# Stick-breaking scores from copies on both row halves, and the conv's last 24 products added by accumulating transfers

## Chip, core and metric

One core of one Trainium2 chip runs the whole program in one launch. The metric is the device time in microseconds (us) of that launch; lower is better. TensorE (PE, with its weight loads PEld), VectorE (DVE), ScalarE (ACT), GpSimd (POOL) and the transfer queue of SyncE (SP) run beside each other and meet only at semaphores.

## What is computed

Two transformer blocks of width 1024 on 512 tokens. The change lies in the mixer of the first block:

```python
# conv branch: 512 channels, 31 taps, causal, depthwise
u = u_val * sigmoid(u_gate)
u = silu(layernorm(causal_depthwise_conv(u, conv_w, conv_b)))
# attention branch, 8 heads of 64
z = (q / 8) @ k.T                       # causal, blocks of 128 queries
log_keep  = where(causal, log_sigmoid(-z), 0)
log_after = cumsum(log_keep, reverse) - log_keep
a = where(causal, exp(log_sigmoid(z) + log_after), 0)
o = a @ v
merged = sigmoid(g_conv) * (u @ w_conv_out) + sigmoid(g_att) * (o @ w_att_out)
```

## The kernel before

All tiles hold features or keys on the 128 partitions and the 512 tokens along the free axis. Nearly every product is made of three matmuls, since each float32 operand is held as a rounded high half and a low rest (`_hi`, `_lo`): high by high, high by low, low by high (`mul`, L1758 to L1761). The engines' orders are written out by hand.

**Weights.** SP issues one 512 KB panel after another in the order of `ITEMS` into three buffers (`raw`, L446). A panel's issue waits until the panel three places before it has been used up. ACT copies a panel to `w_hi` (`prepare`, L584), DVE subtracts to get `w_lo` (`feed`, L1073), and this subtraction frees the buffer. Among the panels from gates 8 on, every gates panel is followed by one panel of `ada`, which DVE multiplies in place (L1067).

**Scores.** `scores(n)` on PE writes the scores of head n for four key blocks: against 512, 384, 256 and 128 queries. First come four small bf16 matmuls that lay down the mask (L1908), then 12 matmuls with 64 partitions of contraction, rows 0 to 63 of the array for an even head and 64 to 127 for an odd one. Head n's queries and keys stand in those partitions of `qk_hi` and `qk_lo`.

**The order in the heads.** PE, in step n: `suffix_sums(n)` (L1928), `stick_out(n-1)` (the product with V), one gates tile, `scores(n+2)`. The last two steps have no scores, and `stick_out(7)` stands at the end, before gates 9 to 15. ACT, in step h: exponential and high half of the weights of head h (`weight`, L701, L705), high half of the output of head h-1 (L630), one `w_hi`, the gates tile out of PSUM (L710), three conv products (L672), then `soft(h+2)` (L690 to L693), which waits for `z_done`. DVE, in step h: `softplus(h+1)` (L1267 to L1273), `feed` of one gates panel (and, late in the heads, an `ada` panel ahead of it), low half of the weights of head h (L1296), low half of the output of head h-1 (`head_lo`, L1278), then conv taps (L1183).

**The conv.** Two of its four channel tiles are made by DVE, one fused multiply-add for each tap (`taps`): 16 beside the q and k projection, 7 beside V, 4 in each head, and the last 7 after the heads, in the step of gates 9. The other two tiles are made by ACT, which writes one product into one of three `tap_buf` (`products`), and POOL, which adds it to `conv` (L494): 33 products before the first head's step, 21 in the heads, 4 after them, 2 at gates 9. After gates 11 PE takes the mean of all four tiles (L1982), and the layer norm follows from there.

Block 2 has the layout that the change brings to block 1 already in its last six score maps (`softmax_scores`, from n = 10): copies of q and k in the other 64 partitions (`q_twin2`, `k_twin2`), brought by POOL's queue, and matmuls on both row halves issued in turn (L2162).

Of the kernel before, what the change touches and what calls it, by code (L numbers as in the profile page):

```python
# [5 lines left out]
P = 128  # L6
D = 1024
SEQ = 512
# [18 lines left out]
WIDE = P * NB * (NB + 1) // 2  # L27
FIRST_ADA = 16
X_ACT = 5
TWIN_FROM = HEADS + 2  # L30
# [72 lines left out]
def build(nc, t):  # L103
# [4 lines left out]
    with ctx:  # L108
# [68 lines left out]
        x_sq = [place(f"x_sq{k}", [P, SEQ], f32, at=A0 + 75 * K + 2 * K * k) for k in range(KT)]  # L177
        qk_hi = place("qk_hi", [P, 8, SEQ], f32r, at=A0)
        qk_lo = place("qk_lo", [P, 8, SEQ], f32r, at=A0 + 16 * K)
        v_hi = place("v_hi", [P, NB, SEQ], f32r, at=A0 + 32 * K)  # L180
# [56 lines left out]
        def sem(name):  # L237
# [19 lines left out]
        glu_done, glu_sig, u_ready = sem("glu_done"), sem("glu_sig"), sem("u_ready")  # L257
        mod_one, mod_ready, pool_tap = sem("mod_one"), sem("mod_ready"), sem("pool_tap")
        tap_prod = sem("tap_prod")
        hi_of = {n: sem(f"hi_of_{n}") for n in ("qk1", "v1", "qk2", "v2", "v3", "qk3")}  # L260
# [6 lines left out]
        out_done_of = {n: sem(f"out_done_{n}") for n in ("ffn_out1", "ffn_out2", "wout_a", "wout_b")}  # L267
        silu_of, prod_of, act_hi_of, act_lo_of = (
            {n: sem(f"{what}_{n}") for n in ("ffn_in1", "ffn_in2")} for what in ("silu", "prod", "act_hi", "act_lo"))
        quad_in = [sem(f"quad_in{i}") for i in range(2)]  # L270
# [21 lines left out]
        lam_dot, lam_exp = sem("lam_dot"), sem("lam_exp")  # L292
        both_in, row_in = sem("both_in"), sem("row_in")
        twin2_in = [sem(f"twin2_in{i}") for i in range(2)]
        s_last = sem("s_last")
# [89 lines left out]
        def _(sp):  # L385
# [25 lines left out]
            def both_halves(n):  # L411
# [10 lines left out]
                for to, src, tile in ((k_both[upper, :], m_hi, k_tile), (k_both[lower, :], m_lo, k_tile),  # L422
                                      (q_both[upper, :], m_hi, q_tile), (q_both[lower, :], m_hi, q_tile)):
                    sp.dma_start(to.bitcast(f32), src[rows, tile, :].bitcast(f32)).then_inc(both_in, 16)

            for q, (name, i) in enumerate(ITEMS):
                if (name, i) in BOTH_AT:
                    both_halves(BOTH_AT[name, i])
                if (name, i) == ("wo", 5):
                    pair_in(0, 0)  # L430
                if (name, i) == ("ffn_in1", 1):
                    sp.wait_ge(mg_c, KT)
                    sp.dma_start(x[:], t["x"]).then_inc(x_again, 16)
# [21 lines left out]
        def _(pool):  # L455
# [34 lines left out]
            for n, (c, j) in enumerate(SUM_ORDER):  # L490
                pool.wait_ge(tap_prod, n + 3)
                if n >= 2:
                    pool.wait_ge(pool_tap, n - 1)
                nc.gpsimd.tensor_tensor(conv[:, c, :], conv[:, c, :], tap_buf[n % 3][:], ALU.add).then_inc(pool_tap, 1)  # L494

# [5 lines left out]

            pool.wait_ge(act_lo_of["ffn_in1"], FT)
            nc.gpsimd.memset(sel_f[:], 0.0).then_inc(consts2, 1)
# [57 lines left out]
        def _(act):  # L561
# [105 lines left out]
            def products(n):  # L667

                for c, j in SUM_ORDER[tapped[0]:tapped[0] + n]:
                    if tapped[0] >= 3:  # L670
                        act.wait_ge(pool_tap, tapped[0] - 2)
                    nc.scalar.activation(tap_buf[tapped[0] % 3][:], u_pad[:, c, j:j + SEQ], ACT.Copy,  # L672
                                         scale=col("conv_w", c * TAPS + j)).then_inc(tap_prod, 1)
                    tapped[0] += 1
# [9 lines left out]
            def soft(h):  # L684
                zb = 3 * (h % 2)
                act.wait_ge(z_done, h + 1)
                if h:
                    act.wait_ge(sp_ready, h)
                for c, lo, up in BY_KEY:
                    nc.scalar.activation(sb_e[:, lo:up], ps[:, zb + c, 0:up - lo], ACT.Abs).then_inc(z_abs, 1)  # L690
                act.wait_ge(z_abs, 3 * (h + 1))
                link(nc.scalar.activation(sb_e[:], sb_e[:], ACT.Exp, scale=-1.0))
                nc.scalar.activation(sb_e[:], sb_e[:], ACT.Ln, bias=1.0).then_inc(z_exp, 1)  # L693
# [95 lines left out]
            def ffn_in(s):  # L789
# [3 lines left out]
                def split(i):  # L793
                    act.wait_ge(prod_of[name], i + 1)
                    nc.scalar.activation(act_hi[:, i, :], act_f[:, i, :], ACT.Copy).then_inc(act_hi_of[name], 1)

# [4 lines left out]
                for i in range(PLAIN):  # L801
# [3 lines left out]
                    used(name, 2 * i)  # L805
                    nc.scalar.activation(t_buf[i % 2][:], ps[:, 2 * i, :], ACT.Silu).then_inc(silu_of[name], 1)
                    prepare(name, 2 * i + 1)
# [237 lines left out]
        def _(dve):  # L1045
# [243 lines left out]
            for h in range(HEADS):  # L1289
# [7 lines left out]
                if h:  # L1297
                    head_lo(h - 1, qk_hi, qk_lo, o_hi, o_ready)
                taps(4)
            head_lo(HEADS - 1, qk_hi, qk_lo, o_hi, o_ready)  # L1300
# [63 lines left out]
            def ffn_in(s):  # L1364
# [4 lines left out]
                def split_lo(i):  # L1369
                    dve.wait_ge(act_hi_of[name], i + 1)  # L1370
                    nc.vector.tensor_tensor(act_lo[:, i, :], act_f[:, i, :], act_hi[:, i, :].bitcast(f32),
                                            ALU.subtract).then_inc(act_lo_of[name], 1)

# [23 lines left out]
                for i in range(PLAIN):  # L1397
# [9 lines left out]
                    dve.wait_ge(silu_of[name], i + 1)  # L1407
                    nc.vector.tensor_tensor(act_f[:, i, :], ps[:, 2 * i + 1, :], t_buf[i % 2][:], ALU.mult)\
                        .then_inc(prod_of[name], 1)
                    if i < 2:  # L1410
# [10 lines left out]
                def product(j):  # L1421
                    dve.wait_ge(part_silu, 2 * (pairs0 + j) + SILU_C21)
                    dve.wait_ge(part_sum, 3 * (pairs0 + j) + C22)
                    nc.vector.tensor_tensor(act_f[:, PLAIN + j, :], up[:], t_buf[j % 2][:], ALU.mult)\
                        .then_inc(prod_of[name], 1)

# [3 lines left out]
                for j in range(BY_SEVEN):  # L1430
# [19 lines left out]
                    dve.wait_ge(part_out, 4 * n + P1_OUT)  # L1450
                    dve.wait_ge(prod_of[name], PLAIN + max(j - 1, 0))
                    nc.vector.tensor_tensor(t_buf[j % 2][:, 0:TOK], ps[:, bank_c, 0:TOK], sq[0][:, 0:TOK], ALU.add)\
# [3 lines left out]
                    dve.wait_ge(part_out, 4 * n + U2_OUT)  # L1456
                    dve.wait_ge(prod_of[name], PLAIN + j)
                    nc.vector.tensor_tensor(up[:, 0:TOK], ps[:, bank_b, 0:TOK], sq[0][:, TOK:SEQ], ALU.add)\
# [9 lines left out]
                product(BY_SEVEN - 1)  # L1468
                dve.wait_ge(prod_of[name], FT)
                link(nc.vector.memset(acc[:], 0.0))  # L1470
# [286 lines left out]
        def _(pe):  # L1757
# [144 lines left out]
            def scores(n):  # L1902
# [15 lines left out]

# [105 lines left out]
            def ffn_in(s, n):  # L2024
# [40 lines left out]

                pe.wait_ge(prod_of[name], 2)
                for j in range(BY_SEVEN):
# [30 lines left out]
            def ffn_out(name, ins_name):  # L2098
                for m in range(KT):
                    for k in range(FT):  # L2100
# [3 lines left out]
                        if m == 0:  # L2104
                            pe.wait_ge(act_lo_of[ins_name], k + 1)
                        if k == 0:
                            pe.wait_ge(prod_of[ins_name], PLAIN if m < 2 else FT)
                        ins = mul(ps[:, OUT_BANK[m], :], panel(name, i, P * part),
# [305 lines left out]
```

## Time and profile before

| | us |
|---|---|
| Median of 3 runs | 1373.14 |
| Lowest, highest of them | 1372.88, 1377.71 |
| The profiled execution | 1373.36 |
| Its span, as the trace has it | 1371.6 |

```profile
PE 1345.3 (98%) x7758; PEld 1168.3 (85%) x7758; DVE 990.5 (72%) x1389; ACT 712.9 (52%) x1167; POOL 176.4 (13%) x165
PE   9999999999999999999999999999999999999997
DVE  6899899678587887878425775667797788776322
POOL 2479333200010000004000011121000000000000
```

The first line gives each engine's busy time, its share of the span and its instructions. The others cut the span into 40 slices of 34 us; a digit is the busy share in tenths, 9 for 90% and more. A matmul's end is modelled in the trace, so the starts of two neighbours say more than their lengths. The chain that ended last is for 82% on PE and for 12% on DVE.

### The profile page before, as it was taken

How to read it: one execution, taken by the hardware profiler on the slowest of the kernel's cores; microseconds unless marked ns; L12 is line 12 of the kernel's file. 1: busy time of each engine (PE TensorE's matmuls, PEld its weight loads, DVE VectorE, ACT ScalarE, POOL GpSimd, SP SyncE). 2: the span in 40 equal slices, each digit the busy share in tenths (PEclk: the TensorE clock that was granted, in tenths of full speed). 3: DMA queues.
4: the chain of work that ended last, by engine and by line, in shares of the span. 5: the costliest groups of instructions: out<-in, count | busy, mean ns of one | idle time of the engine just before them, and what ended most of it. 6: DMA issues, size and time to landing. Idle time of an engine off the chain costs nothing.

```text
span 1371.6 us, 19741 instructions
## 1 busy us (share of the span) xinstructions
PE 1345.3 (98%) x7758; PEld 1168.3 (85%) x7758; DVE 990.5 (72%) x1389; ACT 712.9 (52%) x1167; POOL 176.4 (13%) x165
## 2 busy tenths in 40 slices
PE   9999999999999999999999999999999999999997
PEld 6888887788769999998887778888778999998885
DVE  6899899678587887878425775667797788776322
ACT  3466786563465555564224443557565555564221
POOL 2479333200010000004000011121000000000000
PEclk9999999999999999999999999999999999999998
DMA  9423112456801232224522144543221323223221
GB/s 348 166 81 104 47 47 73 129 185 197 306 16 62 93 116 100 96 105 151 186 94 92 62 138 116 139 112 89 93 77 35 120 93 115 102 108 108 93 92 62
DMA packets 45310, 155.98 MB, mean 114 GB/s; under 512 B 6049, under 2 KB 6305, under 8 KB 45090
## 3 DMA queue, kind: packets, MB, share of 16 engines
q1 hardware_dynamic: 42882, 149.70, 32.8%
q0 software_dynamic: 2336, 5.01, 1.6%
q8 instruction: 62, 1.02, 0.3%
q14 instruction: 30, 0.25, 0.1%
HBM read 143.39 MB, written 2.10 MB: 106 GB/s over the span
## 4 chain that ended last, share of the span: by engine, by line
PE 82%; DVE 12%; ACT 3%; issue 2%; POOL 0%; DVEq 0%; ACTq 0%; POOLq 0%
PE ps L1759 25%; PE ps L1761 25%; PE ps L1760 25%; DVE conv L1183 3%; DVE w_lo L1073 1%; DVE t_buf L1107 1%; PE ps L1851 1%; DVE a_lo L1296 1%; DVE sb_e L1267 1%; PE ps L2194 1%; ACT w_hi L584 1%; PE ps L1805 1%; PE ps L1816 1%; PE ps L1817 1%; PE ps L1821 1%
## 5 line engine op out<-in xcount | busy, mean ns | idle before, releaser
L1759 PE MATMUL ps<-h_hi,w_hi 128*128 128x256 f32 (+1 forms) x1072 | 354.8, 331 | 4.6 <-DVE w_lo L1073 2.2
L1761 PE MATMUL ps<-h_hi,w_lo 128*128 128x256 f32 (+1 forms) x1072 | 352.8, 329 | 0.0
L1760 PE MATMUL ps<-h_lo,w_hi 128*128 128x256 f32 (+1 forms) x1072 | 352.7, 329 | 0.0
L1073 DVE TENSOR_TENSOR w_lo<-raw,w_hi 128x1024 fp32r<-128x1024 f32 x141 | 183.9, 1308 | 113.3 <-ACT w_hi L584 112.6
L1759 PEld LDWEIGHTS ps<-h_hi,w_hi 128*128 128x128 f32 x1072 | 203.8, 190 | 25.5 <-DVE w_lo L1073 3.9
L584 ACT ACTIVATE w_hi<-raw 128x1024 fp32r<-128x1024 f32 x141 | 148.1, 1055 | 144.4 <-PE ps L1761 69.9
L1761 PEld LDWEIGHTS ps<-h_hi,w_lo 128*128 128x128 f32 x1072 | 203.8, 190 | 18.4
L1760 PEld LDWEIGHTS ps<-h_lo,w_hi 128*128 128x128 f32 x1072 | 203.9, 190 | 18.0 <-issue 0.5
L1063 DVE TENSOR_TENSOR w_lo<-quads,w_hi 128x1024 fp32r<-128x1024 f32 (+1 forms) x152 | 164.7, 1085 | 72.8 <-ACT w_hi L584 72.8
L584 ACT ACTIVATE w_hi<-quads 128x1024 fp32r<-128x1024 f32 (+1 forms) x152 | 144.3, 949 | 78.2 <-PE ps L1761 76.5
L1759 PE MATMUL ps<-act_hi,w_hi 128*128 128x512 f32 x352 | 137.0, 389 | 0.0
L1760 PE MATMUL ps<-act_lo,w_hi 128*128 128x512 f32 x352 | 137.0, 389 | 0.0
L1761 PE MATMUL ps<-act_hi,w_lo 128*128 128x512 f32 x352 | 136.9, 389 | 0.0
L1759 PE MATMUL ps<-s_hi,w_hi 128*128 128x256 f32 x456 | 129.0, 283 | 0.0
L1760 PE MATMUL ps<-s_lo,w_hi 128*128 128x256 f32 x456 | 129.0, 283 | 0.0
L1761 PE MATMUL ps<-s_hi,w_lo 128*128 128x256 f32 x456 | 129.0, 283 | 0.0
L494 POOL TENSOR_TENSOR conv<-conv,tap_buf 128x512 f32<-128x512 f32 x60 | 103.1, 1746 | 94.0 <-ACT tap_buf L672 93.7
L1759 PEld LDWEIGHTS ps<-s_hi,w_hi 128*128 128x128 f32 x456 | 87.6, 192 | 0.0
L1760 PEld LDWEIGHTS ps<-s_lo,w_hi 128*128 128x128 f32 x456 | 87.6, 192 | 0.0
L1761 PEld LDWEIGHTS ps<-s_hi,w_lo 128*128 128x128 f32 x456 | 87.6, 192 | 0.0
L815 ACT ACTIVATE sq<-ps 128x256 f32<-128x256 f32 x152 | 57.7, 379 | 45.0 <-PE ps L1761 37.5
L1761 PEld LDWEIGHTS ps<-act_hi,w_lo 128*128 128x128 f32 x352 | 66.1, 188 | 13.8
(339 smaller groups left out, 2333.7 us busy)
## 6 DMA issues: line engine op xcount, KB each, us to landing
quads<-in_ffn_in SPq DMA_DIRECT2D x76, 512.0 KB, 4.4
raw<-in_ffn_out SPq DMA_DIRECT2D x44, 512.0 KB, 3.7
raw<-in_ada SPq DMA_DIRECT2D x32, 512.0 KB, 4.3
raw<-in_qk SPq DMA_DIRECT2D x25, 512.0 KB, 3.7
ada<-in_ada SPq DMA_DIRECT2D x16, 512.0 KB, 7.3
raw<-in_gates SPq DMA_DIRECT2D x16, 512.0 KB, 3.6
raw<-in_v SPq DMA_DIRECT2D x12, 512.0 KB, 3.7
raw<-in_ffn_in SPq DMA_DIRECT2D x12, 512.0 KB, 4.5
```

The costliest lines, as they stand in the source:

```text
L494: nc.gpsimd.tensor_tensor(conv[:, c, :], conv[:, c, :], tap_buf[n % 3][:], ALU.add).then_inc(pool_tap, 1)
L584: nc.scalar.activation(w_hi[SLOT[p]][:, 0:w], src, ACT.Copy).then_inc(hi_ready, 1)
L815: nc.scalar.activation(to, ps[:, bank, 0:TOK], ACT.Copy).then_inc(part_out, 1)
L1063: nc.vector.tensor_tensor(w_lo[SLOT[q]][:, 0:w], src, w_hi[SLOT[q]][:, 0:w].bitcast(f32), ALU.subtract).then_inc(unit_lo, 1)
L1073: nc.vector.tensor_tensor(w_lo[SLOT[p]][:], raw[q % RAW][:], w_hi[SLOT[p]][:].bitcast(f32), ALU.subtract).then_inc(raw_used, 1)
L1107: nc.vector.scalar_tensor_tensor(out=t_buf[k % 2][:], in0=x[:, k, :], scalar=gain_of(k), in1=rstd[:], op0=ALU.mult, op1=ALU.mult).then_inc ...
L1183: ins = nc.vector.scalar_tensor_tensor(out=conv[:, c, :], in0=src, scalar=col("conv_w", c * TAPS + j), in1=conv[:, c, :], op0=ALU.mult, op ...
L1267: nc.vector.scalar_tensor_tensor(out=sb_e[:, lo:up], in0=ps[:, zb + c, 0:up - lo], scalar=0.0, in1=sb_e[:, lo:up], op0=ALU.max, op1=ALU.ad ...
L1296: nc.vector.tensor_tensor(a_lo[:], sb_a[:], a_hi[:].bitcast(f32), ALU.subtract).then_inc(a_ready, 1)
L1759: nc.tensor.matmul(out, w[0], v[0], start=start, stop=False, **kw)
L1760: nc.tensor.matmul(out, w[0], v[1], start=False, stop=False, **kw)
L1761: return nc.tensor.matmul(out, w[1], v[0], start=False, stop=stop, **kw)
```

## The change

Four things are changed.

1. `scores(n)` waits for copies of head n's keys and queries 128 to 511 in the other 64 partitions (`k_twin`, `q_twin`, high and low halves), and issues its 12 matmuls in another order: those of key block 1 (other rows) in turn with those of key block 0 (own rows), then blocks 2 and 3 on the other rows. `z_done` rises twice for each head.
2. SP issues two transfers from SBUF to SBUF for each head, 192 KB each (`twin(h)`), ahead of the panels gates 0 (heads 0 and 1) and gates 5 to 10 (heads 2 to 7). From head 2 on they wait for the scores of head h-2.
3. The last 24 of the 60 products of ACT are added to `conv` by accumulating transfers on POOL's queue instead of POOL additions (`ADDED = 36`: from the first product of the second head step on). The next product into the same `tap_buf` waits for the transfer of the one three places before; a transfer waits for the one two places before, which goes to the same channel tile.
4. DVE takes 5 taps a head instead of 4, so that none is left after the heads.

The rest of the diff joins some semaphores of the feed-forward part into one each, with the counts moved accordingly.

```diff
+ADDED = 36
+TWIN_AT = {0: (0, 1), 5: (2,), 6: (3,), 7: (4,), 8: (5,), 9: (6,), 10: (7,)}
...
+            def twin(h):
+                own, other = slice(HD * (h % 2), HD * (h % 2) + HD), slice(HD - HD * (h % 2), P - HD * (h % 2))
+                sp.wait_ge(lo_of["qk1"], 2 * (h // 2) + 2)
+                if h >= 2:
+                    sp.wait_ge(z_done, 2 * (h - 1))
+                sp.dma_start(k_twin[other, :, :].bitcast(f32), qk_both[own, :, 4 + h // 2, P:SEQ].bitcast(f32))\
+                    .then_inc(twin_in[h % 2], 16)
+                sp.dma_start(q_twin[other, :, :].bitcast(f32), qk_both[own, :, h // 2, P:SEQ].bitcast(f32))\
+                    .then_inc(twin_in[h % 2], 16)
+
             for q, (name, i) in enumerate(ITEMS):
+                if name == "gates":
+                    for h in TWIN_AT.get(i, ()):
+                        twin(h)
...
             for n, (c, j) in enumerate(SUM_ORDER):
                 pool.wait_ge(tap_prod, n + 3)
-                if n >= 2:
+                if n >= ADDED + 2:
+                    pool.wait_ge(tap_sum[n % 2], 16 * ((n - ADDED) // 2))
+                elif n >= 2:
                     pool.wait_ge(pool_tap, n - 1)
-                nc.gpsimd.tensor_tensor(conv[:, c, :], conv[:, c, :], tap_buf[n % 3][:], ALU.add).then_inc(pool_tap, 1)
+                if n < ADDED:
+                    nc.gpsimd.tensor_tensor(conv[:, c, :], conv[:, c, :], tap_buf[n % 3][:], ALU.add)\
+                        .then_inc(pool_tap, 1)
+                else:
+                    nc.gpsimd.dma_start(conv[:, c, :], tap_buf[n % 3][:], accum_op=ALU.add).then_inc(tap_sum[n % 2], 16)
...
-                    if tapped[0] >= 3:
-                        act.wait_ge(pool_tap, tapped[0] - 2)
+                    old = tapped[0] - 3
+                    if old >= ADDED:
+                        act.wait_ge(tap_sum[old % 2], 16 * ((old - ADDED) // 2 + 1))
+                    elif old >= 0:
+                        act.wait_ge(pool_tap, old + 1)
...
-                act.wait_ge(z_done, h + 1)
+                act.wait_ge(z_done, 2 * (h + 1))
...
-                taps(4)
+                taps(5)
...
-                for kb in range(NB):
+                other = rows_of(n + 1)
+                pe.wait_ge(twin_in[n % 2], 32 * (n // 2 + 1))
+                hi_lo = (0, 0), (0, 1), (1, 0)
+                for kb, term in ((1, 0), (0, 0), (1, 1), (0, 1), (1, 2), (0, 2),
+                                 (2, 0), (2, 1), (2, 2), (3, 0), (3, 1), (3, 2)):
                     c, at = KEY_BANK[kb]
                     w = SEQ - P * kb
-                    keys, queries = slice(P * kb, P * (kb + 1)), slice(P * kb, SEQ)
-                    ins = mul(ps[:, 3 * (n % 2) + c, at:at + w],
-                              (qk_hi[rows, 4 + n // 2, keys], qk_lo[rows, 4 + n // 2, keys]),
-                              (qk_hi[rows, n // 2, queries], qk_lo[rows, n // 2, queries]), False, True, **free)
-                ins.then_inc(z_done, 1)
+                    a, b = hi_lo[term]
+                    if kb == 0:
+                        key = qk_both[rows, a, 4 + n // 2, 0:P]
+                        query = qk_both[rows, b, n // 2, :]
+                    else:
+                        key = k_twin[other, a, P * (kb - 1):P * kb]
+                        query = q_twin[other, b, P * (kb - 1):SEQ - P]
+                    ins = nc.tensor.matmul(ps[:, 3 * (n % 2) + c, at:at + w], key, query, start=False, stop=term == 2,
+                                           **free)
+                    if term == 2 and kb in (0, 3):
+                        ins.then_inc(z_done, 1)
...
                     pe.wait_ge(tap, len(TAP_ORDER))
-                    pe.wait_ge(pool_tap, len(SUM_ORDER))
+                    for i in range(2):
+                        pe.wait_ge(tap_sum[i], 16 * ((len(SUM_ORDER) - ADDED) // 2))
```

## Rows read from the trace of the kernel before

**Rows 1.** Busy us by engine in stretches; last columns clock, DMA share, GB/s

```profile
139.50:239.00 99.50, 96.97 (x549) 83.97 (x548) 93.88 (x95) 76.18 (x111) 35.87 (x21) 1.00 0.17 55
```

**Rows 2.** Timeline of PE: start, length, line, operands; the scores of two heads

```profile
200.71 0.40 PE L1908 MATMUL ps<-mask_kq,ident_b 128*128 128x128 bf16 x4
201.04 0.50 PE L1759 MATMUL ps<-qk_hi 64*128 64x512 f32 x1
203.09 0.50 PE L1928 MATMUL ps<-sb_hi,tri 128*128 128x512 f32 x1
...
213.34 0.40 PE L1908 MATMUL ps<-mask_kq,ident_b 128*128 128x128 bf16 x4
```

**Rows 3.** Timeline of PE: its only two waits in the heads

```profile
229.71 0.47 PE L1759 MATMUL ps<-a_hi,v_hi 128*128 128x512 f32 x1 [0.86 <-DVE qk_lo L1278]
...
239.13 0.47 PE L1759 MATMUL ps<-a_hi,v_hi 128*128 128x512 f32 x1 [1.79 <-DVE qk_lo L1278]
```

**Rows 4.** Timeline of DVE in the heads

```profile
208.12 1.62 DVE L1267 SCALAR_TENSOR_TENSOR sb_e<-ps,sb_e 128x512 f32<-128x512 f32 x3
...
212.12 1.22 DVE L1073 TENSOR_TENSOR w_lo<-raw,w_hi 128x1024 fp32r<-128x1024 f32 x1
...
215.25 5.91 DVE L1183 SCALAR_TENSOR_TENSOR conv<-u_pad,cols,conv 128x512 f32<-128x512 f32 x4
...
234.51 1.22 DVE L1067 SCALAR_TENSOR_TENSOR raw<-raw,c_all 128x1024 f32<-128x1024 f32 x1
...
238.91 2.72 DVE L1183 SCALAR_TENSOR_TENSOR conv<-u_pad,cols,conv 128x512 f32<-128x512 f32 x4
```

**Rows 5.** Timeline of POOL in the heads

```profile
214.82 5.14 POOL L494 TENSOR_TENSOR conv<-conv,tap_buf 128x512 f32<-128x512 f32 x3 [7.94 <-ACT tap_buf L672]
```

**Rows 6.** Timeline of PE in block 2: score map 9 on one row half, map 10 on both

```profile
922.26 0.32 PE L1759 MATMUL ps<-m_both 64*128 64x128 f32 x1
...
925.17 0.47 PE L1759 MATMUL ps<-pt_hi,v_hi 128*128 128x512 f32 x1
...
930.25 0.49 PE L2162 MATMUL ps<-m_both 64*128 64x512 f32 x1
...
932.07 0.50 PE L1759 MATMUL ps<-m_both,w_hi 128*128 128x512 f32 x1
```

**Rows 7.** Timeline of the SP queue: V panel 3, and the ada panel behind gates 9

```profile
107.09 0.33 SPq L446 DMA_DIRECT2D raw<-in_v  x1
...
213.36 0.33 SPq L446 DMA_DIRECT2D raw<-in_ada  x1
```

**Rows 8.** Timeline of PE: the mask of head 0

```profile
109.79 0.40 PE L1908 MATMUL ps<-mask_kq,ident_b 128*128 128x128 bf16 x4
```

**Rows 9.** DMA issues of the whole run: queue, count, KB each, median us to landing

```profile
raw<-in_v SPq DMA_DIRECT2D x12, 512.0 KB, 3.7
...
q_both<-m_both SPq DMA_DIRECT2D x16, 128.0 KB, 3.9
...
k_twin<-m_both POOLq DMA_DIRECT2D x6, 192.0 KB, 3.1
```

**Rows 10.** Timeline of ACT: in head step 4, and behind the last head

```profile
200.91 0.60 ACT L710 ACTIVATE gate_c<-ps 128x512 f32<-128x512 f32 x1 [2.07 <-PE ps L1761]
...
203.24 1.34 ACT L690 ACTIVATE sb_e<-ps 128x512 f32<-128x512 f32 x3
...
207.10 1.34 ACT L701 ACTIVATE sb_a<-ps 128x512 f32<-128x512 f32 x3
...
241.89 1.95 ACT L672 ACTIVATE tap_buf<-u_pad,cols 128x512 f32<-128x512 f32 x3
```

**Rows 11.** Timeline of PE behind the heads: gates 9 begins, and the conv's mean

```profile
241.07 0.45 PE L1759 MATMUL ps<-h_hi,w_hi 128*128 128x512 f32 x1
...
257.47 3.60 PE L1982 MATMUL ps<-conv,ones_d 128*128 128x512 f32 x8
```

**Rows 12.** Busy us by engine near the start, columns as in the first group

```profile
9.00:13.00 4.00, 4.00 (x12) 2.56 (x13) 3.10 (x5) 3.98 (x8) 0.60 (x1) 0.57 1.03 417
```

More of the change, by code:

```diff
@@ L177, in build @@
         x_sq = [place(f"x_sq{k}", [P, SEQ], f32, at=A0 + 75 * K + 2 * K * k) for k in range(KT)]
-        qk_hi = place("qk_hi", [P, 8, SEQ], f32r, at=A0)
-        qk_lo = place("qk_lo", [P, 8, SEQ], f32r, at=A0 + 16 * K)
+        qk_both = place("qk_both", [P, 2, 8, SEQ], f32r, at=A0)
+        qk_hi, qk_lo = qk_both[:, 0, :, :], qk_both[:, 1, :, :]
+        q_twin = place("q_twin", [P, 2, SEQ - P], f32r, at=A0 + 63 * K)
+        k_twin = place("k_twin", [P, 2, SEQ - P], f32r, at=t_at + 5 * K)
         v_hi = place("v_hi", [P, NB, SEQ], f32r, at=A0 + 32 * K)
@@ L258, in build @@
         mod_one, mod_ready, pool_tap = sem("mod_one"), sem("mod_ready"), sem("pool_tap")
+        tap_sum = [sem(f"tap_sum{i}") for i in range(2)]
         tap_prod = sem("tap_prod")
@@ L267, in build @@
         out_done_of = {n: sem(f"out_done_{n}") for n in ("ffn_out1", "ffn_out2", "wout_a", "wout_b")}
-        silu_of, prod_of, act_hi_of, act_lo_of = (
-            {n: sem(f"{what}_{n}") for n in ("ffn_in1", "ffn_in2")} for what in ("silu", "prod", "act_hi", "act_lo"))
+        silu, prod, act_hi_s, act_lo_s = sem("silu"), sem("prod"), sem("act_hi_s"), sem("act_lo_s")
+        PAIRS_AT = {"ffn_in1": 0, "ffn_in2": FT}
         quad_in = [sem(f"quad_in{i}") for i in range(2)]
@@ L293, in build @@
         both_in, row_in = sem("both_in"), sem("row_in")
+        twin_in = [sem(f"twin_in{i}") for i in range(2)]
         twin2_in = [sem(f"twin2_in{i}") for i in range(2)]
@@ L500, in _ @@
                 nc.gpsimd.tensor_tensor(x[:, k, :], x[:, k, :], t_buf[k // 2 % 2][:], ALU.add).then_inc(x_even, 1)
-            pool.wait_ge(act_lo_of["ffn_in1"], FT)
+            pool.wait_ge(act_lo_s, FT)
             nc.gpsimd.memset(sel_f[:], 0.0).then_inc(consts2, 1)
@@ L793, in split @@
                 def split(i):
-                    act.wait_ge(prod_of[name], i + 1)
-                    nc.scalar.activation(act_hi[:, i, :], act_f[:, i, :], ACT.Copy).then_inc(act_hi_of[name], 1)
+                    act.wait_ge(prod, PAIRS_AT[name] + i + 1)
+                    nc.scalar.activation(act_hi[:, i, :], act_f[:, i, :], ACT.Copy).then_inc(act_hi_s, 1)
                 def sum_hi(n):
@@ L805, in ffn_in @@
                     used(name, 2 * i)
-                    nc.scalar.activation(t_buf[i % 2][:], ps[:, 2 * i, :], ACT.Silu).then_inc(silu_of[name], 1)
+                    nc.scalar.activation(t_buf[i % 2][:], ps[:, 2 * i, :], ACT.Silu).then_inc(silu, 1)
                     prepare(name, 2 * i + 1)
@@ L1369, in split_lo @@
                 def split_lo(i):
-                    dve.wait_ge(act_hi_of[name], i + 1)
+                    dve.wait_ge(act_hi_s, PAIRS_AT[name] + i + 1)
                     nc.vector.tensor_tensor(act_lo[:, i, :], act_f[:, i, :], act_hi[:, i, :].bitcast(f32),
-                                            ALU.subtract).then_inc(act_lo_of[name], 1)
+                                            ALU.subtract).then_inc(act_lo_s, 1)
                 def sum_lo(n):
@@ L1406, in ffn_in @@
                     dve.wait_ge(panel_used, FIRST[name] + 2 * i + 2)
-                    dve.wait_ge(silu_of[name], i + 1)
+                    dve.wait_ge(silu, PLAIN * s + i + 1)
                     nc.vector.tensor_tensor(act_f[:, i, :], ps[:, 2 * i + 1, :], t_buf[i % 2][:], ALU.mult)\
-                        .then_inc(prod_of[name], 1)
+                        .then_inc(prod, 1)
                     if i < 2:
@@ L1424, in product @@
                     nc.vector.tensor_tensor(act_f[:, PLAIN + j, :], up[:], t_buf[j % 2][:], ALU.mult)\
-                        .then_inc(prod_of[name], 1)
+                        .then_inc(prod, 1)
                 dve.wait_ge(s_hi_of, 4 * s + 4)
@@ L1450, in ffn_in @@
                     dve.wait_ge(part_out, 4 * n + P1_OUT)
-                    dve.wait_ge(prod_of[name], PLAIN + max(j - 1, 0))
+                    dve.wait_ge(prod, PAIRS_AT[name] + PLAIN + max(j - 1, 0))
                     nc.vector.tensor_tensor(t_buf[j % 2][:, 0:TOK], ps[:, bank_c, 0:TOK], sq[0][:, 0:TOK], ALU.add)\
@@ L1456, in ffn_in @@
                     dve.wait_ge(part_out, 4 * n + U2_OUT)
-                    dve.wait_ge(prod_of[name], PLAIN + j)
+                    dve.wait_ge(prod, PAIRS_AT[name] + PLAIN + j)
                     nc.vector.tensor_tensor(up[:, 0:TOK], ps[:, bank_b, 0:TOK], sq[0][:, TOK:SEQ], ALU.add)\
@@ L1468, in ffn_in @@
                 product(BY_SEVEN - 1)
-                dve.wait_ge(prod_of[name], FT)
+                dve.wait_ge(prod, PAIRS_AT[name] + FT)
                 link(nc.vector.memset(acc[:], 0.0))
@@ L2064, in last_product @@
                     part(ps[:, banks_of(j)[0], first], u, 0, a22, False).then_inc(panel_used, 1)
-                pe.wait_ge(prod_of[name], 2)
+                pe.wait_ge(prod, PAIRS_AT[name] + 2)
                 for j in range(BY_SEVEN):
@@ L2104, in ffn_out @@
                         if m == 0:
-                            pe.wait_ge(act_lo_of[ins_name], k + 1)
+                            pe.wait_ge(act_lo_s, PAIRS_AT[ins_name] + k + 1)
                         if k == 0:
-                            pe.wait_ge(prod_of[ins_name], PLAIN if m < 2 else FT)
+                            pe.wait_ge(prod, PAIRS_AT[ins_name] + (PLAIN if m < 2 else FT))
                         ins = mul(ps[:, OUT_BANK[m], :], panel(name, i, P * part),
```

## The prediction, made before the changed kernel ran

> **What bounds the kernel now.** I read the busy shares first, then the stretch of the heads, then PE's and DVE's timelines of one head, and last SP's queue, because the change puts transfers there. PE is busy throughout, so only what shortens or stops PE moves the end. In the heads PE is busy for 96.97 of 99.50 us and DVE for 93.88: two engines run nearly full side by side [rows 1]. PE's head takes 12.63 us from mask to mask (213.34 - 200.71) and no idle time is printed between [rows 2]; its only waits are 0.86 and 1.79 us, at the end of the heads, where DVE is late [rows 3]. DVE is late because four taps take 5.91 us beside POOL's additions and 2.72 us alone [rows 4, 5]. So PE sets the pace, DVE follows closely, and DVE's lateness costs 2.65 us once.
>
> **Scores, 8 heads.** One head's 12 matmuls run from 201.04 to 203.09: 2.05 us [rows 2]. Block 2 shows what two row halves give. Map 9, 5120 columns on one half, takes 925.17 - 922.26 = 2.91 us. Map 10 has 3072 of them on the busier half and takes 932.07 - 930.25 = 1.82 us [rows 6]. The busier half of the new order has 3 x (384 + 256 + 128) = 2304 columns of 3840. In proportion to columns the two maps give 2.05 x 2304/3840 = 1.23 and 1.82 x 2304/3072 = 1.37 us; the short matmuls of 128 columns do not shrink in full, so I take 1.43. That saves 0.62 a head, 0.5 to 0.8 at the ends, and **5.0 us** for 8 heads. The masks stay.
>
> **Taps and additions.** Without POOL's additions five taps cost 5 x 0.68 = 3.4 us where four cost up to 5.91 [rows 4], so DVE gains about 2 us a head and is no longer close behind. The first wait of 0.86 goes. The second goes in part: behind the last suffix sums ACT still makes high half, output half and a panel half, and DVE a panel's low half, the weights' low half and the output's low half, in series, while PE has the product of head 6 and one gates tile. What goes is the time the `ada` product (1.22 us, at 234.51 [rows 4]) stood in front of that chain, about 1.0; 0.8 to 0.9 of the wait stays. Saved: **1.9 us** (1.0 to 2.65). The 7 taps behind the heads now end before PE's mean is due, but PE did not wait for them, so that is worth nothing.
>
> The Trainium skill, SBUF — State Buffer, section "SBUF: two separate sides", speaks against moving this to POOL's queue: descriptors of a transfer from that queue are written by GpSimd and cannot be written while DVE runs a copy that holds the shared ports. No row here has an accumulating transfer. By that rule each transfer could start later by DVE's copy in `softplus`, which would add to the landing time weighed below; without it nothing is added.
>
> **New wait 1, scores(0).** Its two copies stand on SP behind V panel 3, issued at 107.09 and 0.33 us long [rows 7]. The first copy is issued at about 107.4, the second near 108.05. The second lands 3.1 us (the like copy on POOL's queue) to 3.9 us (four copies in series on SP's queue) later [rows 9]: 111.15 to 111.95; the panel ahead of it lands at 107.09 + 3.7 = 110.8 and so excludes much less. PE is ready at 109.79 + 0.33 = 110.1 [rows 8]. Behind the waiting matmul stand V's product, the first gates tile and scores(1), all without slack, so the wait counts in full: 1.0 to 1.9; with the panel's data in front I take **1.8 us**.
>
> **New wait 2, scores(7).** The copies of head 7 stand ahead of gates 10, and so behind the `ada` panel that is issued at 213.36, just after DVE's low half of gates 8, which starts at 212.12 and takes 1.22 us [rows 4, 7]. PE's mask for scores(7) is at 213.34 [rows 2]. So they are issued when they are already due. In the new kernel, counted from the end E of scores(6): ACT takes the gates tile and three products before `soft(6)`, from 200.91 to 203.24 = 2.33 us behind the end of a gates tile, which is E - 1.75, with 0.2 us before it starts: E + 0.75. `soft` takes 207.10 - 203.24 = 3.86 [rows 10], DVE's softplus 212.12 - 208.12 = 4.0, the panel's low half 1.22 [rows 4]. The `ada` panel is issued at E + 9.9, the copies at E + 10.3 and E + 10.9, and the second lands at E + 14.0 to 14.8. PE is there at 213.34 - 203.09 + 0.33 = E + 10.6 [rows 2]. The wait is 3.4 to 4.2, up to 5.5 if the copies move slowly behind 512 KB; I take **4.0 us**. The suffix sums of head 6, a product with V and a gates tile stand behind it. For heads 2 to 6 the copies are issued 8 us and more ahead of need, since the panel in front of each is issued an earlier head before: nothing.
>
> **The accumulating transfers.** Let L be the time from a product to its sum in `conv`. In the heads the third product of a head needs the third transfer of the head before: 0.72 + 2L has to be under 13.3, so L under 6.3, and ACT has 2 us idle a head beyond that [rows 10]. Behind the heads the limit is tighter. Counted from the start of gates 9 (241.07) the products start at 0.8 (241.89) and the mean stands at 16.4 (257.47) [rows 10, 11]. The last products form three transfers in series, since each waits for the one two before, and each buffer for the one three before: the last lands at about 2.25 + 3L. That is under 16.4 for L up to 4.7; above, every us of L costs 3. Nearest rows: a copy of 192 KB on POOL's queue lands in 3.1 us [rows 9]; an accumulation also has to read what it adds to, so at most about twice that, 6.2. I take 4.0, nearer to the copy: **nothing**, with ends 0 and +4.5. The skill's DMA: Bandwidth & Descriptors, section "Anatomy of one DMA — SWDGE (gpsimd) path", has a fixed 2.0 us plus bytes over 436 GB/s for a plain transfer, an estimate of 2.6 us for 256 KB; by that the sum is unchanged too.
>
> **Sum.** -5.0 - 1.9 + 1.8 + 4.0 = **-1.1 us**. From the profiled execution's 1373.36 (span 1371.6) that gives 1372.3; that execution lies 0.2 above the median, so against 1373.14 it is 1372.0. I give 1372.2. PE runs without a gap from the heads to 360 us, and what follows is counted from PE, so the shift reaches the end unchanged. Half a per cent, about what can be told from no change here, is 6.9 us.
>
> **Rivals.**
> A, *the copies are there in time* (they overtake, or DVE frees the buffers much earlier than I reckon): no new waits, all of both gains, -5.0 - 2.65 = -7.6: 1365.6. Against it: SP's order is fixed, and the `ada` panel ahead of them hangs on scores(6).
> B, *the accumulations take over the bound*, on the other side. Place: the mean behind gates 11, and from L = 6.3 ACT's third product in each head. At L = 6.2 the mean costs 2.25 + 18.6 - 16.4 = +4.5: 1376.6. At L = 8 it costs 9.9, and in five heads 16.7 - 13.3 less 2 us of idle time = 1.4 each: +17, 1388. It makes a slower kernel by over 0.5% from L = 7. For it: no row shows such a transfer, and three in series have no slack to share. Against: POOL's plain copies land in 3.1.
> C, *the clock falls in the wait of 4 us* and PE resumes at half speed. Near the start the granted clock averaged 0.57 over 9 to 13 us, after a stretch of few one-partition matmuls; those 4 us lost 1.7 [rows 12]. The same again gives +1.7 - 1.1 = +0.6: 1373.8. The skill's TensorE: Matmul & The Clock Gate, section "HAM oscillation — how this bites in real kernels", has waits for a transfer throwing the array back to its low level; the short waits of this trace show none.
> D, *the halves do not overlap*: no 5.0, so +3.9: 1377.1. Against it stands map 10.
>
> **How the numbers follow.** Forecast 0.55 (its own range 1369.5 to 1375.5), A 0.10, B 0.18 (of it 0.11 beyond L = 7), C 0.14, D 0.03. The low end lies between the forecast's and A's, 1367.5; the high end takes in B up to L = 6.2 with a longer wait 2, 1380. Faster by over 0.5%: most of A, 0.08. Slower: B beyond L = 7 and mixtures, 0.14. Within: 0.78.
>
> **What would show it.** Scores near 1.43 us from first matmul to suffix sums; four to five taps at 0.7 us each; a PE wait near 1.8 us at scores(0) and near 4 at scores(7), both ended by a transfer into `q_twin`; no wait at the V product of head 6 and one under 1 us at that of head 7; no wait before the mean. A wait of ACT's products or of PE's mean on POOL's queue is B; a granted clock under 1.00 behind 210 us is C. I am wrong if scores(7) doesn't wait, or if L exceeds 4.7.

## The result and the profile after

The changed kernel takes 1385.62 us (median of 4 runs, 1384.11 to 1390.43) against 1373.39 before (median of 4). The ratio is 1.0099, 95% interval 1.0081 to 1.0117: slower by 1.0%. The prediction was 1372.2, between 1367.5 and 1380.0, so it missed by 13 us on the side to which it gave 0.14.

The profiled execution of the changed kernel took 1390.43 us, span 1388.7, and is the longest of the four; 2.7 us of that lie ahead of the first changed instruction, where profiled executions of all these kernels differ by up to 4.4 us. The granted clock goes with it: over the first 20 us it lost 3.4 us in this trace, 1.7 in the trace of before and nothing in that of `a_early`, which reaches the first mask earliest, at 108.05. (What the clock loses in a stretch is 1 minus the granted clock, times the length of the stretch.) Cut at three marks of PE's timeline, the two spans compare like this (us; the kernel with both repairs is run `e_best` below):

| From, to | Before | After | Both repairs |
|---|---|---|---|
| Start to first score mask | 109.8 | 112.5 | 110.4 |
| First mask to gates 9 | 131.3 | 139.8 | 124.2 |
| Gates 9 to the conv's mean | 16.4 | 20.5 | 16.4 |
| Mean to the end | 1114.1 | 1115.9 | 1114.2 |

So the loss is in the heads (8.5) and in front of and just behind the mean (5.9). First what was meant to be gained. PE's timeline of a head, columns as in the rows of before:

```profile
170.04 0.40 PE L1936 MATMUL ps<-mask_kq,ident_b 128*128 128x128 bf16 x4
170.37 0.44 PE L1952 MATMUL ps<-q_twin,k_twin 64*128 64x384 f32 x1
170.37 0.49 PE L1952 MATMUL ps<-qk_both 64*128 64x512 f32 x1
...
171.74 0.50 PE L1966 MATMUL ps<-sb_hi,tri 128*128 128x512 f32 x1
...
181.98 0.40 PE L1936 MATMUL ps<-mask_kq,ident_b 128*128 128x128 bf16 x4
```

Two matmuls start at 170.37 on different rows; the scores take 171.74 - 170.37 = 1.37 us where they took 2.05, and a head takes 11.94 us instead of 12.63 [rows 2]. DVE's taps are as short as without GpSimd's additions, 3.39 us for five [rows 4]:

```profile
173.98 3.39 DVE L1211 SCALAR_TENSOR_TENSOR conv<-u_pad,cols,conv 128x512 f32<-128x512 f32 x5
```

Now every place from 100 to 300 us where PE's timeline prints a wait for another engine or a transfer:

```profile
116.26 0.69 PE L1952 MATMUL ps<-q_twin,k_twin 64*128 64x384 f32 x1 [3.41 <-DMA q_twin<-qk_both]
...
223.77 0.68 PE L1952 MATMUL ps<-q_twin,k_twin 64*128 64x384 f32 x1 [5.58 <-DMA q_twin<-qk_both]
250.34 0.47 PE L1787 MATMUL ps<-a_hi,v_hi 128*128 128x512 f32 x1 [0.81 <-DVE qk_both L1306]
272.80 5.37 PE L2021 MATMUL ps<-conv,ones_d 128*128 128x512 f32 x8 [3.96 <-DMA conv<-tap_buf]
```

The waits of 0.86 and 1.79 us [rows 3] have become one of 0.81. Three new ones stand there: 3.41 at the scores of head 0, 5.58 at those of head 7, 3.96 at the conv's mean, 12.95 us together. And behind each the granted clock (the third column from the right) falls to 0.50, the lower of its two levels, 1.2 GHz:

```profile
114.00:116.00 2.00, 0.00 (x0) 0.00 (x0) 2.00 (x3) 1.98 (x3) 2.00 (x2) 1.00 0.94 193
116.00:118.00 2.00, 1.74 (x9) 1.74 (x10) 2.00 (x2) 1.52 (x2) 2.00 (x2) 0.56 0.83 263
118.00:120.00 2.00, 2.00 (x8) 1.69 (x7) 2.00 (x2) 1.20 (x3) 1.84 (x2) 0.50 0.03 10
120.00:122.00 2.00, 2.00 (x6) 1.52 (x6) 1.58 (x2) 1.94 (x3) 0.00 (x0) 0.50 0.18 16
122.00:124.00 2.00, 2.00 (x8) 1.58 (x7) 0.00 (x0) 0.76 (x1) 0.00 (x0) 0.74 0.69 242
...
222.00:224.00 2.00, 0.23 (x2) 0.23 (x4) 0.89 (x2) 0.00 (x0) 0.00 (x0) 0.51 1.11 205
224.00:226.00 2.00, 2.00 (x12) 2.00 (x12) 0.00 (x0) 0.00 (x0) 0.62 (x1) 0.50 0.27 47
...
230.00:232.00 2.00, 2.00 (x10) 1.90 (x10) 1.62 (x3) 0.65 (x2) 0.00 (x0) 0.50 0.00 0
232.00:234.00 2.00, 2.00 (x14) 1.84 (x13) 1.94 (x2) 1.01 (x4) 0.00 (x0) 0.93 0.00 0
...
274.00:276.00 2.00, 2.00 (x4) 0.76 (x3) 0.00 (x0) 0.00 (x0) 0.00 (x0) 0.50 0.44 166
```

PE's busy time counts slow matmuls in full, so it hides this loss. The clock lost 2 x (0.44 + 0.50 + 0.50 + 0.26) = 3.4 us behind the first wait, about 4.2 over the 8.3 us from 223.8 to 232.1 behind the second. Heads: 3.41 + 5.58 + 3.4 + 4.2 - 8 x 0.68 - (2.65 - 0.81) = +9.3 against 8.5 measured.

Why the transfers are late can be read from SP's queue, by the same columns:

```profile
109.76 0.33 SPq L465 DMA_DIRECT2D raw<-in_v  x1
110.13 0.70 SPq L437 DMA_DIRECT2D k_twin<-qk_both  x1
110.88 0.60 SPq L439 DMA_DIRECT2D q_twin<-qk_both  x1
...
217.61 0.33 SPq L465 DMA_DIRECT2D raw<-in_ada  x1
218.06 0.60 SPq L437 DMA_DIRECT2D k_twin<-qk_both  x1
218.70 0.61 SPq L439 DMA_DIRECT2D q_twin<-qk_both  x1
```

They are issued where the prediction put them: behind V panel 3, and behind the `ada` panel when they are already due (head 7's mask is at 217.79). Head 0's second copy, issued at 110.88, ends PE's wait at 116.26, 5.4 us later; head 7's, at 218.70, does so at 223.77, 5.1 later. The other second copies issued right behind a panel took 4.7, 7.2 and 5.9 us to land as well (heads 2, 5 and 6); PE needed those later and did not wait.

### The profile page after: what moved, and what is told of

It is laid out like the page before. It is cut to its first block, busy times and chain, and to the rows that moved or that the text cites. A ratio compares the mean times of both kernels' runs of the same rounds, so it can differ in the third digit from the quotient of the medians.

```text
span 1388.7 us, 19763 instructions
## 1 busy us (share of the span) xinstructions
PE 1350.7 (97%) x7758; PEld 1171.0 (84%) x7758; DVE 973.0 (70%) x1389; ACT 713.0 (51%) x1167; POOL 157.1 (11%) x165
## 4 chain that ended last, share of the span: by engine, by line
PE 75%; issue 10%; DVE 6%; DMA 4%; ACT 3%; POOL 2%; DVEq 0%; POOLq 0%; ACTq 0%
PE ps L1787 23%; PE ps L1788 23%; PE ps L1789 23%; DMA conv<-tap_buf 4%; POOL conv L516 1%; DVE t_buf L1135 1%; PE ps L2233 1%; PE ps L1879 1%; DVE w_lo L1101 1%; ACT w_hi L609 1%; PE ps L1833 1%; PE ps L1891 1%; PE ps L1844 1%; PE ps L1845 1%; PE ps L1849 1%
## 5 line engine op out<-in xcount | busy, mean ns | idle before, releaser
L1787 PEld LDWEIGHTS ps<-act_hi,w_hi 128*128 128x128 f32 x352 | 66.1, 188 | 13.7
```

Source lines behind the costliest of these rows:

```text
L1787: nc.tensor.matmul(out, w[0], v[0], start=start, stop=False, **kw)
```

## Experiments

Two explanations stood after this reading. One: late transfers stop PE, and each stop costs again through the clock. The other: the change puts so much on the transfer engines and POOL's queue that the time would come back elsewhere if a wait were removed. All ratios are to runs of the kernel before on the same chip, with their 95% interval. The runs fall into four sets; the kernel before had medians from 1372.06 to 1373.39 in them, so the medians of two kernels from different sets compare to about 1 us.

**a_early: the two late pairs of copies issued earlier.**

```diff
-TWIN_AT = {0: (0, 1), 5: (2,), 6: (3,), 7: (4,), 8: (5,), 9: (6,), 10: (7,)}
+TWIN_AT = {("v1", 2): (0,), ("gates", 0): (1,), ("gates", 5): (2,), ("gates", 6): (3,), ("gates", 7): (4,), ("gates", 8): (5,), ("gates", 9): (6, 7)}
```

> The changed kernel with only the place of four copies moved on SyncE's queue: head 0's ahead of V panel 2 and head 7's beside head 6's, ahead of gates 9. Theory (each late copy stops TensorE and the stop also halves its clock for a while): the waits of 3.4 us at the scores of head 0 and 5.6 us at those of head 7 go, and with them half of the 6.4 and 8.3 us in which the granted clock stood at 0.50 behind them, so 3.4 + 3.2 + 5.6 + 4.2 = 16.4 us off 1385.6: 1369. The wait at the conv's mean stays near 4 us. Rival (the transfers as such crowd the queues, and the time returns elsewhere): the waits go but under 5 us are gained, 1381 or more.

Measured: 1372.38 us, ratio 1.0003 (0.9988 to 1.0018). 13.2 us come back: both waits and what the clock took behind them. The clock is 1.00 from 100 to 239 us. One wait of over 1 us is left:

```profile
253.52 2.05 PE L2020 MATMUL ps<-conv,ones_d 128*128 128x512 f32 x2 [4.64 <-DMA conv<-tap_buf]
```

In the two traces the stretch from the first mask to gates 9 went from 139.8 to 124.2 us, 15.6 less and near the 16.4 expected; the medians give 13.2. The changed kernel's profiled execution had lost more to the clock (0.988 on average) than its other runs (0.990 to 0.992), which goes in the right direction; how the clock went in those others is not recorded.

**b_fill: the waits stay, the array is kept busy in them.**

```diff
+                busy(3 * (n % 2), {0: 14, 7: 24}.get(n, 0))
...
+                    busy(CV_MEAN, 17)
```

> The changed kernel with idle-time matmuls of 128 columns in front of the three waits of TensorE: 14 before the scores of head 0, 24 before those of head 7, 17 before the conv's mean (about 3.0, 5.2 and 3.7 us). The waits for the data stay; only the array is kept busy in them. Theory (the low clock behind the waits costs time of its own): granted clock 1.00 behind all three, and the 3.2 + 4.2 + 1.6 = 9 us lost at half clock come back, 1377. Rival (what runs at half clock is hidden behind other engines): unchanged, 1385.6 give or take 2.

Measured: 1380.93 us, 1.0063 (1.0048 to 1.0078), 4.7 us less than the changed kernel. The waits are there in full: 14 matmuls (3.0 us) and then 0.61 more at head 0, 24 (5.2) and 0.39 at head 7, 17 (3.7) and 0.41 at the mean; the clock is 1.00 from 100 to 300 us, and 0.996 on average in three of four runs. So the low clock is a cost of its own. Its size is less certain: 4.7 us in the medians, half of what I expected, but about 8 in the pair of traces. There the stretch up to the mean is 6.3 us shorter (160.4 to 154.1, counted from the fill ahead of the first mask), and behind the mean 1.8 are gained, of which the clock takes 1.7 back between 808 and 814 us.

**c_last_pool: the six sums behind the heads on GpSimd again.** A helper `summed(n)` names the semaphore and the count of sum n.

```diff
+ADDED_TO = 54
...
-                if n < ADDED:
+                if not ADDED <= n < ADDED_TO:
```

> The changed kernel with the last six of the 24 sums, those behind the heads, added by GpSimd again; the 18 in the heads stay accumulating transfers. Theory (three transfers in series behind the heads are what the conv's mean waits for): no wait at the mean, 4.0 us less, and 1.6 us less at half clock behind it: 1380. Rival (the mean would wait for something else, taps or a panel): the wait stays within 1 us of 4.

Measured: 1379.98 us, 1.0052 (1.0037 to 1.0067): 5.6 us less, as expected. The mean stands 16.4 us behind gates 9 again (245.87 to 262.26), without a wait.

**d_no_accum: all sums on GpSimd, copies and 5 taps kept** (`ADDED = 60`).

> The changed kernel with all 60 sums added by GpSimd, and the 5 taps a head and the copies kept. Theory (GpSimd's additions slow VectorE's taps and would make it the bound once TensorE's head is shorter): a tap takes about 1.35 us in the heads instead of 0.68, VectorE needs 4.0 + 1.2 + 1.5 + 0.7 + 6.7 = 14.1 us a head where TensorE has 11.94, so about 2.1 us a head over six heads are lost, 12 us, against 5.6 us gained at the mean: 1392. Rival (TensorE stays the bound): 1380.

Measured: 1386.91 us, 1.0104 (1.0089 to 1.0119). The direction is right and the size 5 us too high. DVE's head takes 13.1 us: five taps take 4.85 us, not 6.7, but the low half of the weights takes 2.59 instead of 1.48, since GpSimd's additions now fall upon it. PE waits on DVE at the V products of five of the eight heads (0.59 to 1.90 us), and longer for head 7's copies (7.67).

```profile
179.57 2.59 DVE L1326 TENSOR_TENSOR a_lo<-sb_a,a_hi 128x1280 fp32r<-128x1280 f32 x1
```

This trace also shows that shorter waits can draw the clock down. Behind the wait of 1.90 us it fell to 0.50, and behind one of 2.65 us at head 0 too (at 0.50 or near it from 114 to 118 us); behind the four waits of 0.59 to 1.24 it stayed at 1.00.

```profile
252.74 0.47 PE L1789 MATMUL ps<-a_hi,v_hi 128*128 128x512 f32 x1 [1.90 <-DVE qk_both L1308]
...
254.00:256.00 2.00, 2.00 (x10) 1.89 (x9) 1.25 (x3) 0.61 (x2) 0.00 (x0) 0.53 0.09 37
```

**e_best: both repairs** (a_early and c_last_pool).

> Both repairs at once: the copies of heads 0 and 7 issued earlier, and the last six sums on GpSimd again (18 accumulating transfers stay in the heads). Theory (two late copies and one serial chain of transfers are all that the change loses): no wait over 1 us on TensorE in the heads and none at the mean, so 4.6 us of wait and about 1.6 us at half clock less than with the early copies alone, 1372.4 - 6.2 = 1366.2, and 0.5% faster than the kernel before. Rival (the 13 us regained by the early copies hold also what the mean cost): 1370 to 1372.

Measured: 1366.79 us (5 runs, 1364.74 to 1366.92), 0.9957 (0.9945 to 0.9970): faster than both kernels, and 0.6 us from the forecast. PE's only waits from 100 to 300 us:

```profile
224.24 0.47 PE L1788 MATMUL ps<-a_hi,v_hi 128*128 128x512 f32 x1 [0.34 <-DVE qk_both L1307]
232.67 0.47 PE L1788 MATMUL ps<-a_hi,v_hi 128*128 128x512 f32 x1 [0.82 <-DVE qk_both L1307]
```

It settles the question between the two explanations: nothing came back elsewhere. From the first mask to the mean it is 7.1 us shorter than before, 8 x 0.68 = 5.4 from the scores and 2.65 - 1.16 = 1.5 from DVE.

**f_early_no_accum: the early copies, all sums on GpSimd.**

> The early copies, 5 taps a head, and all 60 sums on GpSimd; no accumulating transfer. Against the run with both repairs this prices the 18 transfers in the heads. Theory (the shorter scores are worth something only if VectorE keeps up): VectorE's head takes 13.2 us as in the run without transfers, against 11.94 of TensorE, six heads lose about 1.2 us each, so 7 us more than with both repairs, about 1373. Rival (TensorE hides it): 1366 to 1368.

Measured: 1379.40 us, 1.0052 (1.0038 to 1.0066): 12.6 us more than e_best, where I expected 7. With 5 taps a head, the 18 transfers in the heads are worth more than the 5.4 us of the shorter scores. Without them the shorter scores bring nothing: h_no_copies_no_accum below, which has neither copies nor transfers and the same 5 taps, takes 1378.73. The early copies with 4 taps and without transfers were not run, so how much of the 12.6 us the fifth tap makes is open. PE now waits on DVE for 9.7 us in eight places, the longest behind the last head with scores:

```profile
234.52 0.47 PE L1788 MATMUL ps<-a_hi,v_hi 128*128 128x512 f32 x1 [3.67 <-DVE qk_both L1307]
...
236.00:238.00 2.00, 2.00 (x9) 1.94 (x9) 2.00 (x4) 0.20 (x1) 0.00 (x0) 0.50 0.00 0
```

That wait too drew the clock down.

**g_no_copies: transfers and 5 taps, scores as before.** (`TWIN_AT = {}`, and `scores` with the 12 matmuls of before.)

> The changed kernel without the copies: scores as before on one row half, no transfers of q and k; 24 accumulating transfers and 5 taps a head stay. Theory: TensorE's head is 12.63 us again, the waits on VectorE of 0.86 and 1.79 shrink to 0.8 in all, and the wait at the mean of about 4.5 us stays with 1.6 us at half clock: 1373 - 1.9 + 6.1 = 1377. Rival (the transfers are slow only beside the copies): no wait at the mean, 1371.

Measured: 1380.54 us, 1.0065 (1.0050 to 1.0081). The wait at the mean is 4.36 us without any copy in the program, so the rival that blamed them falls. The 3.5 us above the forecast are a larger loss of the clock: mean to end takes 1120.0 us against 1114.1. In the four rows from 256 to 264 us (0.63, 0.50, 0.50, 0.66) the clock loses 3.4, about 2.6 of it behind the mean, which starts at 258.21. Another 3.4 are lost far from the change, in block 2, from 802 to 810 us; two of the four rows:

```profile
804.00:806.00 2.00, 2.00 (x6) 1.49 (x6) 1.35 (x2) 0.62 (x2) 0.00 (x0) 0.50 0.14 57
806.00:808.00 2.00, 2.00 (x6) 1.61 (x5) 1.69 (x7) 0.87 (x4) 0.01 (x1) 0.50 0.00 0
```

At this place PE waits 0.8 us for DVE in the traces of before and after, too. The clock fell behind it in those of g_no_copies and c_last_pool (3.4 us each) and of b_fill and i_plain (1.7 each), and in none of the others. So single executions differ by up to 3.4 us there, whatever the change does.

**h_no_copies_no_accum: the kernel before with 5 taps.** Of the change only `taps(5)` acts here, with the joined semaphores of the feed-forward part.

> The kernel before with 5 taps a head instead of 4 and nothing else: no copies, all sums on GpSimd. Theory (VectorE becomes the bound): its head takes 13.2 us against 12.63 of TensorE, six heads lose 0.6 us each, 3.5 us, and nothing is gained behind the heads: 1377. Rival (the fifth tap fits in idle time): 1373.

Measured: 1378.73 us, 1.0049 (1.0035 to 1.0063), 6.7 us slower. The fifth tap alone lets DVE fall behind: in the trace PE's waits on DVE grow from 2.65 to 5.67 us, 3.67 of them at the V product of head 6, and behind that one the clock loses 3.4.

**i_plain: a_early with transfers that copy instead of adding.**

```diff
-                    nc.gpsimd.dma_start(conv[:, c, :], tap_buf[n % 3][:], accum_op=ALU.add).then_inc(tap_sum[n % 2], 16)
+                    nc.gpsimd.dma_start(conv[:, c, :], tap_buf[n % 3][:]).then_inc(tap_sum[n % 2], 16)
```

> The kernel with the early copies and all 24 transfers, but the transfers only copy the product over the sum instead of adding it, so the conv's two upper channel tiles lose their sums. It prices the adding. Theory (the landing time hangs on what else is on the transfer engines, not on the adding): alone in a head the third transfer still takes 3.2 to 3.7 us, the last two behind the heads, beside panels of 512 KB, 6 to 7, and the wait at the mean stays at 3.5 to 4.6. Rival (adding makes them slow): landings near 2.6 to 3, wait at the mean under 1.

Measured: 1366.91 us, 0.9959 (0.9946 to 0.9972), no wait at the mean. My theory fell here: adding does cost. The page's issue lists, first the changed kernel's, then this one's:

```profile
conv<-tap_buf POOLq DMA_DIRECT2D x24, 256.0 KB, 4.5
```

```profile
conv<-tap_buf POOLq DMA_DIRECT2D x24, 256.0 KB, 3.3
```

A transfer that adds lands 1.2 us later in the median, and POOL issues it in 0.85 us instead of 0.54. The mean waits for a chain of three, the second, fourth and sixth sum behind the heads. They landed in 6.2, 3.5 and 7.9 us in a_early and in 3.8, 2.3 and 6.2 here: 5.3 us less in all, more than a_early's wait of 4.64. The last one, issued behind two panels of 512 KB, takes 6.2 even as a plain copy, so what else is on the transfer engines seems to count too; no run took the panels away.

**j_early_fill: a_early with 21 idle-time matmuls ahead of the mean.**

> The kernel with the early copies, and 21 idle-time matmuls (4.5 us) ahead of the conv's mean, so that TensorE has no idle stretch there. Only the low clock behind the one wait left is taken away. Theory: granted clock 1.00 from 239 to 300 us instead of 0.97, and 1.6 us less than 1372.4: 1370.8. Rival (nothing of it is on the path): 1372.4.

Measured: 1371.51 us, 0.9992 (0.9980 to 1.0003), and the clock is 1.00 from 239 to 300 us in its profile. 0.9 us less than a_early is in the expected direction and within what such runs scatter; this run alone decides nothing.

**k_head7_only: only head 7's copies moved.**

> The changed kernel with only head 7's copies moved, beside head 6's ahead of gates 9; head 0's stay late. Theory (each late copy costs its wait and about half of a stretch at 0.50 behind it): 13.2 us were regained by moving both; head 7's share is its wait of 5.6 and half of the clock that the idle-time matmuls gave back, about 8, head 0's 5. So 1385.6 - 8 = 1377.6. Rival (the waits overlap in effect, one takes over what the other leaves): under 4 us gained.

Measured: 1380.62 us, 1.0054 (1.0037 to 1.0070). By the medians head 7's copies are worth 5.0 us and head 0's the other 8.2, where I had expected 8 and 5. The traces say the opposite and come near what I had expected. Against a_early's 124.2 us, the stretch from the first mask to gates 9 is 2.7 longer here, where only head 0's copies are late, and 15.6 longer in the trace of after, where 6.6 fall between the first and the second mask, to head 0, and the other 9.0 to head 7. In c_last_pool, with the same late copies, it is 4.9 and 7.2. So the split of the medians is not to be trusted; the sum of both, 12 to 16 us, is. In the profiled execution the wait at head 0 was 2.65 us, the clock stayed at 1.00 behind it, and it took 1375.5 us at a mean clock of 0.995. The other five took 1379.7 to 1382.7 at 0.991 to 0.994: the same code is 4 to 7 us slower at a lower mean clock. Where in those five the clock fell was not traced.

```profile
113.00 0.44 PE L1951 MATMUL ps<-q_twin,k_twin 64*128 64x384 f32 x1 [2.65 <-DMA q_twin<-qk_both]
...
114.00:116.00 2.00, 2.00 (x12) 1.67 (x11) 2.00 (x2) 2.00 (x4) 2.00 (x2) 1.00 0.63 240
```

**l_four_taps: e_best with 4 taps a head.**

> The kernel with both repairs, but 4 taps a head and the last 7 behind the heads, as before the change. Theory (VectorE has slack once 18 of the sums are gone from GpSimd, and the taps behind the heads end before the mean): no difference, 1366.8 give or take 1.5. Rival (the taps behind the heads hold the mean or the panels back, now that TensorE comes 6 us earlier): 1368.5 or more.

Measured: 1366.16 us, 0.9954 (0.9938 to 0.9970), the same as e_best. The fifth tap is worth nothing once DVE has slack. From the mean to the end its trace takes 1114.1 us, as the kernel before does, so the joined semaphores cost nothing there either.

## Why the prediction was wrong

**The work itself was right.** Scores 1.37 us against 1.43, 5.4 saved against 5.0; taps 0.68 each; the wait at the V product of head 6 gone (0.34 of it is back in e_best, where no late copy stands in front) and 0.81 left at head 7's against "0.8 to 0.9"; the tap moved into the heads worth nothing (l_four_taps). Gains of 7.3 us were there.

**Both new waits at the copies were found, and mis-sized.** The step that failed is the landing time. I took 3.1 to 3.9 us, medians of [rows 9]; behind a panel of 512 KB and beside each other the second copies took 5.3 and 5.0. The trace of before had such a value: the slowest of the six copies of `k_twin`.

```profile
DMA to landing us min/median/max: 2.9/3.1/5.4
```

The trace of after shows both prices in one kernel. Time to landing of the second copy of heads 0 and 1 (issued behind V panel 3) and of head 3 (issued with nothing in front):

```profile
DMA to landing us min/median/max: 5.1/5.2/5.3
...
DMA to landing us min/median/max: 2.9/2.9/2.9
```

Waits of 3.4 and 5.6 instead of 1.8 and 4.0: 3.2 us of the miss. For head 7 I had 5.5 us as the upper end and named this reason; taking the middle was the error. For head 0 my upper end was 1.9, so there the range itself was wrong, although I had reckoned with the panel in front.

**The sums behind the heads.** Rival B, at 0.18, had the place and the sum right (2.25 + 3L against 16.4); the step that failed is L = 4.0, "nearer to the copy". Time to landing in the changed kernel's trace, of the first and second sum behind the heads, of the fourth and of the sixth:

```profile
DMA to landing us min/median/max: 4.0/5.1/6.3
...
DMA to landing us min/median/max: 3.6/3.6/3.6
...
DMA to landing us min/median/max: 7.0/7.0/7.0
```

The mean starts 20.5 us behind gates 9, so L was (20.5 - 2.25) / 3 = 6.1 on average, near my upper end of 6.2, for which I had written +4.5; the wait was 3.96. The chain is the second, fourth and sixth sum, 6.3 + 3.6 + 7.0 = 16.9 us of landing; what is missing to three times 6.1 is the time between a landing and the next issue. The adding alone accounts for the wait (i_plain). That the first and the last of the three are slow because of the panels beside them is argued from the times of issue and not shown by a run. Repairing this alone gave 5.6 us (c_last_pool). A slip besides: slower by over 0.5% needs +8.0 us at the mean, so L = 7.4 and not 7, and L = 8 gives 1389, not 1388.

**The clock.** Rival C had 0.14 and 1.7 us for one wait. It happened behind all three, and I had reckoned it as an alternative to the forecast where it is a follow-up of every wait. Its price is 4.7 us in the medians (b_fill) and about 8 in the two traces. The Trainium skill, TensorE: Matmul & The Clock Gate, section "HAM oscillation — how this bites in real kernels", which the prediction cites, has the fall come again with every such wait for a transfer. The traces agree, with 3.4, 4.2 and 1.7 us lost behind the three. The trace of before could not tell: behind its longest wait in these stages, 1.79 us, the clock stayed at 1.00.

**Together.** Waits beyond the forecast 1.6 + 1.6 + 4.0 = 7.2, clock 4.7, less 0.4 of larger gains: 11.5 of the 13.4 us by which 1385.6 exceeds 1372.2. About 1.9 us stay unassigned. The wait at head 0 and the clock's part lay outside their stated ends, the wait at head 7 and L at them. All erred on the same side: all three landings were slower than the medians I took, and the clock followed each wait. The range's high end, 1380, had room for slow sums and a longer wait at head 7 together, but not for head 0 and the clock on top.

## What to carry to other kernels

A transfer's landing time has to be taken from rows with the same company on the transfer engines; right behind a 512 KB load the second copy took 4.7 to 7.2 us, with nothing right in front 2.9. Where a copy is issued by a queue that also waits for buffers, read which wait stands in front of it: moving two of the eight pairs of copies ahead by two panels each turned a loss of 12 us into equality, and six sums taken back off a serial chain made the version that beats both kernels. And a wait on TensorE of 3 us or more was never only that wait in these traces: price the low clock behind it with it.

## What the hardware showed that I had not expected

- Behind waits of TensorE of 3.2 to 7.7 us, for a transfer or for DVE, the granted clock stood at or near 0.50 for 3 to 14 us. Behind shorter ones it went either way: behind 2.65 us it fell in d_no_accum and stayed at 1.00 in k_head7_only, behind 1.90 us it fell (d_no_accum), behind 1.79 it did not (before), and behind the same 0.8 us in block 2 it fell in four of the fourteen traces.
- A sum of 128x512 f32 by an accumulating transfer landed in 3.2 us at best, 4.5 in the median and 7.6 at worst, and took POOL 0.85 us to issue; the plain copy had 2.3, 3.3 and 7.0, and 0.54. In eight of the traces with accumulating transfers, DVE's copy of 128x1280 (L1300 in after) began while POOL was issuing one, and that issue took 1.05 to 1.45 us. The prediction had weighed such a delay by this copy; at up to 0.6 us, once or twice a run, it decided nothing.
- The low half of the weights (`a_lo`, 128x1280) took 1.48 us alone and 2.59 when a GpSimd addition fell upon it. In the kernel before the two never met. The fifth tap is enough to make them meet: h_no_copies_no_accum has the scores of before and shows 2.59 too.
